# Who makes the low parts of the weight chunks: GpSimd, or VectorE from the first gated v chunk on

## The chip, the cores and the metric

One core of a Trainium2 chip runs the whole program in one launch. The metric is the device time of that launch in microseconds; the kernel before was timed three times.

## What is computed

`x` is 256 tokens by 1024 (fp32). Two layers of a first block run, then two layers of a second. Only the end of the second block's layer matters here, the feed-forward part with learned experts:

```python
def chunk(xc):                       # 128 tokens at a time
    q = (xc @ w_q).reshape(c, PEER_HEADS, 2, PEER_HALF)
    sc = jnp.einsum('chpd,hpnd->chpn', q, sub_keys)
    ...                              # top 16 of 128 keys per half, then top 16 of the 256 pairs
    gate = jax.nn.softmax(best_s, axis=-1)
    act = jax.nn.gelu(jnp.einsum('chkd,cd->chk', u_tab[idx], xc))
    return jnp.einsum('chk,chkd->cd', gate * act, v_tab[idx])
```

There are 128 x 128 experts, each with a row of `u_tab` and of `v_tab` (1024 numbers each), 8 heads and 16 experts a head and token.

## The kernel before, in words

**No gathering.** The kernel doesn't fetch the chosen experts. It computes all 16,384 hidden values of every token densely, in 128 blocks of 128 experts, multiplies them by a gate that is zero where an expert was not chosen, and multiplies the result with all of `v_tab`. Block n needs a *u chunk* (128 x 1024, way in) and a *v chunk* (128 x 1024, way out).

**Three products for one.** Each fp32 operand is kept as a high part (rounded to the type that TensorE reads) and a low part (the rest), and a product is three matmuls: high by high, high by low, low by high (`mm3`). So each of the 800 weight chunks of 512 KB goes through: SyncE loads it into one of `RAW2` = 4 slots of `raw` (L462, by `load_layer`), ScalarE copies it to `w_hi` (L1077, class `Split`), GpSimd subtracts to get `w_lo` (L572, `split_layer`), TensorE uses both. Counting semaphores order this: `w_ready` (loaded), `hi_ready`, `lo_ready`, `w_used` (TensorE is done with n chunks). A raw slot is loaded again once `lo_ready` says that its low part is made; a pair of slots (`PAIR2` = 4) is written again once `w_used` says so. In the trace `w_hi` and `w_lo` are both named `w_split`.

**The order of chunks** in a layer of the second block: the first `N2_PRE` chunks are for projections and queries; then 48 u chunks (`STASH`), whose hidden values go, through Gelu, to a stash (`stash_in`) while VectorE still works on the top 16; then, from chunk `N2_OUT` on, 48 v chunks for these blocks; then, for blocks 48 to 127, u and v chunks in turn, each u one block ahead of its v (`run_base`, `_stream2`).

**The stages of the way out** (`RUNS`, L1308, L1927 and TensorE's `hidden_blocks`, L716):
- blocks 0 to 47 use the stash: one v chunk a block, and beside it one group of one-hots;
- blocks 48 to 95: a u and a v chunk, and one group of one-hots;
- blocks 96 to 127: a u and a v chunk.

**One block, engine by engine.** VectorE first makes a group of one-hots for gates that are needed 32 blocks later (`onehots`, L1900: `one_j` 256 wide, `one_i` 1024 wide, three `gate_j` 256 wide, all bf16), then in `gated` (L1420) the product of hidden values and gate twice (L1428 in fp32, L1429 as `hidw_hi`) and their difference `hidw_lo` (L1431). `gated` waits for `hid_ready` (Gelu done) and for `w_used` (the block two before is through). TensorE, in each turn of `one_pass`, computes the way in of the next block (24 matmuls of 256 columns, L656), a gate group (24 small matmuls, L997, out of the one-hots) and the way out of this block (12 matmuls of 512 columns, L656), which waits for `hidw_ready`. ScalarE makes the high parts of the next u and this v chunk, the Gelu (L1121) and a copy of the gates (L1279). The order of each engine is written out by hand in loops of its own, four blocks to a turn. GpSimd does nothing else in them than to split.

**GpSimd's part** is one program of its own, `split_layer(n, raws, pairs, pause, between)`: it goes through all `n` = `N2` chunks of the layer, in order, and waits for the matching counts. The rest of a layer's small work for GpSimd is done at chunk `pause`.

The lines that say it:

```python
pool.wait_ge(hi_ready, c + 1)
if at >= pairs:
    pool.wait_ge(w_used, c - pairs + 1)
pool.tensor_tensor(w_lo[at % pairs], raw[:, at % raws, :], w_hi[at % pairs].bitcast(F32),
                   ALU.subtract).then_inc(lo_ready, 1)
```

Of the kernel before, what the change touches and what calls it, by code (L numbers as in the profile page):

```python
# [22 lines left out]
F32 = mybir.dt.float32  # L23
# [4 lines left out]
ALU = mybir.AluOpType  # L28
# [29 lines left out]
NK = 128  # L58
# [9 lines left out]
N2_MIX = 13 + 4 + 1  # L68
N2_PRE = N2_MIX + 8 + 16
STASH = 48  # L70
N2_OUT = N2_PRE + STASH

RUNS = ((0, JQ), (JQ, STASH - JQ), (STASH, 2 * JQ - STASH), (2 * JQ, JQ), (3 * JQ, JQ))
N2 = N2_PRE + 2 * NK
RAW1, PAIR1 = 3, 6
RAW2, PAIR2 = 4, 4
EARLY = 3
AHEAD = 2
# [9 lines left out]
def run_base(first):  # L88

    return N2_OUT + first if first < STASH else N2_PRE + 2 * first  # L90

# [59 lines left out]
def two_blocks_kernel(nc, x_in, pos_in, stream, col1, row1, col2, row2, small2, sub2, inv_in, out):  # L151
# [4 lines left out]
    with ExitStack() as ctx:  # L156
# [10 lines left out]
        raw = sb("raw", [P, max(RAW1, RAW2), CH])  # L167
        RING = max(PAIR1, PAIR2)
        w_split = sb("w_split", [P, 2 * RING, CH], F32R)
        w_hi = [w_split[:, k, :] for k in range(RING)]  # L170
# [359 lines left out]
        def _(pool):  # L530
# [35 lines left out]
            def split_layer(n, raws, pairs, pause, between):  # L566

                def one(c, at):
# [6 lines that stand above are left out]
                turn = max(raws, pairs)  # L575
                head = max(turn, pause)
                head += (n - head) % turn
                for c in range(head):
                    if between is not None and c == pause:
                        between()  # L580
                    one(c, c)
                if between is not None and pause == head:
                    between()
                with pool.Fori(0, (n - head) // turn) as i:
                    for k in range(turn):
                        one(i * turn + (head + k), head + k)
# [35 lines left out]
            second_constants()  # L622
            with pool.Fori(0, DEPTH) as l:
                enter_layer(pool, "pool", l + (1 + DEPTH))
                split_layer(N2, RAW2, PAIR2, N2_MIX + AHEAD, mix_norm)
                leave_layer(pool, "pool", lo_ready, N2)

        CONSTS = 4
# [722 lines left out]
        def _(dve):  # L1351
            V = nc.vector
# [67 lines left out]
            def gated(i, unroll, u, done, base, ups, value, gate, free):  # L1420

                s = u % 2
                dve.wait_ge(hid_ready, i * unroll + (done + u + 1))
                if free:

                    first = isinstance(i, int) and i == 0 and u < 2
                    dve.wait_ge(w_used, base + u - 1 if first else i * (unroll * (ups + 1)) + (base + (ups + 1) * (u - 1) + ups))
                V.tensor_tensor(gated_hid[:, s, :], value, gate, ALU.mult).then_inc(gate_step, 1)  # L1428
                V.tensor_tensor(hidw_hi[:, s, :], value, gate, ALU.mult).then_inc(gate_step, 1)  # L1429
                dve.wait_ge(gate_step, i * (2 * unroll) + 2 * (done + u + 1))  # L1430
                V.tensor_tensor(hidw_lo[:, s, :], gated_hid[:, s, :], hidw_hi[:, s, :].bitcast(F32),  # L1431
                                ALU.subtract).then_inc(hidw_ready, 1)
# [185 lines left out]
            def layer_norm(step, n, full, dst, g, b, stats, mean_var, std, rstd, signal):  # L1618

                half = lambda c: slice(c * 512, (c + 1) * 512)  # L1620
                for count, banks in full:
                    dve.wait_ge(out_full, count)
                    for t, c in banks:
                        step(V.scalar_tensor_tensor(out=dst[:, t, half(c)], in0=x_res[:, t, half(c)], scalar=ALPHA,
                                                    in1=acc[2 * t + c], op0=ALU.mult, op1=ALU.add))
                    step.settle()
                    for t, c in banks:
                        step(V.bn_stats(stats[:, t, c, :], dst[:, t, half(c)]))
                step.settle()
                for t in range(TT):  # L1630
                    step(V.bn_aggr(mean_var[:, t, :], stats[:, t].rearrange("p c s -> p (c s)")))
                root_of(step, n)
                step(V.reciprocal(rstd, std))
                step.settle()
                for t in range(TT):
                    step(V.scalar_tensor_tensor(out=dst[:, t, :], in0=dst[:, t, :], scalar=mean_var[:, t, 0:1], in1=g,
                                                op0=ALU.subtract, op1=ALU.mult))
                    step.settle()
                    ins = V.scalar_tensor_tensor(out=x_res[:, t, :], in0=dst[:, t, :], scalar=rstd[:, t:t + 1], in1=b,
                                                 op0=ALU.mult, op1=ALU.add)  # L1640
                    if signal is not None:
                        ins.then_inc(signal, 1)
                    else:
                        step(ins)

            def block2():
# [253 lines left out]
                def onehots(n, i, step, free):  # L1900

                    if free:
                        dve.wait_ge(onehot_used, i * step + (n - 1))
                    s, q = n % 2, n // JQ
                    at = i * (step * GROUP) + n % JQ * GROUP
                    tokens = slice(at, at + GROUP) if isinstance(i, int) else bass.ds(at, GROUP)
                    pairs = lambda x: x.rearrange("p (c k) -> p c k", k=2)
                    shape = lambda keys: [P, GROUP // 2, keys, 2]
                    keys = iota_b[:, q * JQ:(q + 1) * JQ, :]
                    V.tensor_tensor(one_j[:, s], keys.unsqueeze(1).broadcast_to(shape(JQ)),  # L1910
                                    pairs(i2T[:, tokens]).unsqueeze(2).broadcast_to(shape(JQ)),
                                    ALU.is_equal).then_inc(onehot_step, 1)
                    V.tensor_tensor(one_i[:, s], iota_b[:].unsqueeze(1).broadcast_to(shape(NK)),  # L1913
                                    pairs(i1T[:, tokens]).unsqueeze(2).broadcast_to(shape(NK)),
                                    ALU.is_equal).then_inc(onehot_step, 1)
                    dve.wait_ge(onehot_step, i * (2 * step) + 2 * (n + 1))
                    for m in range(PIECES):
                        ins = V.tensor_tensor(gate_j[:, s, :, m], one_j[:, s],  # L1918
                                              pairs(g_part[:, m, tokens]).unsqueeze(2).broadcast_to(shape(JQ)), ALU.mult)
                    ins.then_inc(onehot_ready, 1)  # L1920

                for u in range(8):
                    onehots(u, 0, 8, u >= 2)
                with dve.Fori(1, JQ // 8) as i:
                    for u in range(8):
                        onehots(u, i, 8, True)
                for first, n in RUNS:  # L1927
                    def one(i, u, free):
                        if first < NK - JQ:
                            onehots(JQ + first + u, i, 4, True)  # L1930
                        j = i * 4 + (first % JQ + u)
                        b = i * 4 + (first % JQ + u)
                        if first >= STASH:
                            value = hid[:, u % 2, :]
                        elif isinstance(b, int):
                            value = stash[first // JQ][:, b, :]
                        else:
                            value = stash[first // JQ][:, bass.ds(b, 1), :].rearrange("p b t -> p (b t)")
                        gated(i, 4, u, first, run_base(first), int(first >= STASH), value, gates[:, first // JQ % 2, :, j], free)

                    if first % JQ == 0:
                        dve.wait_ge(gates_out, first + JQ)
                    for u in range(4):
                        one(0, u, first > 0 or u >= 2)
                    with dve.Fori(1, n // 4) as i:
                        for u in range(4):
                            one(i, u, True)
                layer_norm(step, 6, [(LAST_SUMS - TT + t + 1, [(t, c) for c in range(2)]) for t in range(TT)], ypre,
                           par("ln2_g"), par("ln2_b"), bn3, mv3, std3, rstd3, None)
                return step.n  # L1950
# [122 lines left out]
```

## Time and profile before

| | |
|---|---|
| times of three runs | 3289.58, 3296.64, 3299.37 us |
| median | 3296.64 us |
| span of the profiled execution | 3291.1 us |
| TensorE matmuls busy | 2821.9 us (86%) |
| VectorE busy | 2427.6 us (74%), 3941 instructions |
| GpSimd busy | 2063.1 us (63%), of which 2028.4 us are the 800 splits |
| ScalarE busy | 1233.0 us (37%) |
| granted TensorE clock, mean over the span | 0.918 |
| read from HBM | 429 MB, 131 GB/s over the span |

The span runs from the first to the last instruction of one profiled execution; the three times are of runs of their own, their median 5.5 us above that span. Busy time counts an instruction from its start to its end, so one that stands still inside it counts as busy. The granted clock is a share of the full 2.4 GHz and is a mean of two levels, 1.2 and 2.4 GHz. A share over the whole span mixes stages with different limits, so the rows further down go stage by stage. "Idle before" in a row, in brackets, is the wait of the engine just before the instruction and who ended it.

### The profile page before, as it was taken

The numbers are of one execution on the slowest core, as the hardware profiler recorded it, in microseconds if no ns is written. First come the engines' busy times: TensorE is split into PE (matmuls) and PEld (weight loads), VectorE is DVE, ScalarE is ACT, GpSimd is POOL, SyncE is SP. The second block draws the span as 40 slices with busy tenths as digits, with TensorE's granted clock in tenths as the row PEclk, the third lists the DMA queues.
The fourth block names the chain that finished last, engine by engine and source line by source line (L and its number), as shares of the span: only waits on it lengthen the run. The fifth ranks groups of instructions, "written<-read, shape, count | busy, mean of one in ns | idle before, by whom it ended". The sixth has DMA issues, their size and how long they took to land.

```text
span 3291.1 us, 62310 instructions
## 1 busy us (share of the span) xinstructions
PE 2821.9 (86%) x21856; PEld 2498.9 (76%) x21856; DVE 2427.6 (74%) x3941; ACT 1233.0 (37%) x1814; POOL 2063.1 (63%) x849
## 2 busy tenths in 40 slices
PE   6899888999799777788888898789777788888897
PEld 6689877898589766568777787679765567777786
DVE  8521383313859999989999665849999989999766
ACT  4444343443435332223333343344432223333343
POOL 6378673887268544457667786357744447666786
PEclk9999997999699988789999999789998889999999
DMA  4145341555144322234434454224332224444453
GB/s 170 58 163 189 138 149 56 178 183 206 39 141 166 104 95 96 96 103 141 141 140 138 156 172 179 90 97 168 120 103 96 94 85 141 141 140 140 145 175 121
DMA packets 118027, 432.35 MB, mean 131 GB/s; under 512 B 13952, under 2 KB 13952, under 8 KB 117376
## 3 DMA queue, kind: packets, MB, share of 16 engines
q1 hardware_dynamic: 117888, 430.43, 37.8%
q8 instruction: 96, 1.57, 0.2%
q14 instruction: 43, 0.35, 0.0%
HBM read 429.33 MB, written 1.05 MB: 131 GB/s over the span
## 4 chain that ended last, share of the span: by engine, by line
PE 42%; DVE 37%; issue 16%; ACT 2%; DVEq 1%; POOL 1%; DMA 0%; SPq 0%; ACTq 0%; POOLq 0%
PE ps L656 40%; DVE hidw_hi L1429 7%; DVE hidw_lo L1431 5%; DVE gate_j L1918 4%; DVE one_i L1913 2%; DVE one_j L1910 2%; DVE arena L1428 2%; PE ps L997 2%; DVE arena L1852 1%; DVE arena L1874 1%; DVE arena L1877 1%; DVE arena L1844 1%; DVE arena L1837 1%; DVE arena L1838 1%; DVE arena L1495 1%
## 5 line engine op out<-in xcount | busy, mean ns | idle before, releaser
L572 POOL TENSOR_TENSOR w_split<-raw,w_split 128x1024 fp32r<-128x1024 f32 x800 | 2028.4, 2550 | 1008.5 <-ACT w_split L1077 1006.2
L656 PE MATMUL ps<-hT_hi,w_split 128*128 128x256 f32 x6688 | 1264.1, 286 | 22.9 <-POOL w_split L572 16.9
L1077 ACT ACTIVATE w_split<-raw 128x1024 fp32r<-128x1024 f32 x800 | 841.2, 1060 | 872.8 <-PE ps L656 698.6
L656 PEld LDWEIGHTS ps<-hT_hi,w_split 128*128 128x128 f32 x6688 | 1070.4, 193 | 39.3 <-POOL w_split L572 13.4
L656 PE MATMUL ps<-w_split,hidw_hi 128*128 128x512 f32 x2400 | 842.1, 434 | 186.8 <-DVE hidw_lo L1431 186.3
L656 PE MATMUL ps<-hT_lo,w_split 128*128 128x256 f32 x3344 | 952.0, 285 | 0.0
L656 PEld LDWEIGHTS ps<-w_split,hidw_hi 128*128 128x128 f32 x2400 | 470.9, 206 | 295.2 <-DVE hidw_lo L1431 129.4
L656 PEld LDWEIGHTS ps<-hT_lo,w_split 128*128 128x128 f32 x3344 | 646.2, 193 | 8.2
L1431 DVE TENSOR_TENSOR hidw_lo<-arena,hidw_hi 128x256 fp32r<-128x256 f32 x300 | 502.7, 1676 | 10.3
L656 PE MATMUL ps<-w_split,hidw_lo 128*128 128x512 f32 x1200 | 508.1, 423 | 0.0
L1918 DVE TENSOR_TENSOR gate_j<-one_j,arena 128x256 bf16<-128x256 bf16 x768 | 389.6, 561 | 31.4
L1428 DVE TENSOR_TENSOR arena<-arena 128x256 f32<-128x256 f32 (+1 forms) x224 | 179.0, 799 | 182.6 <-ACT arena L1121 167.5
L656 PEld LDWEIGHTS ps<-w_split,hidw_lo 128*128 128x128 f32 x1200 | 246.9, 206 | 62.0
L1429 DVE TENSOR_TENSOR hidw_hi<-arena 128x256 fp32r<-128x256 f32 (+1 forms) x224 | 283.0, 1263 | 0.0
L997 PEld LDWEIGHTS ps<-gate_j,one_i 128*128 128x128 bf16 x6144 | 172.8, 98 | 124.7 <-DVE gate_j L1918 73.9
L997 PE MATMUL ps<-gate_j,one_i 128*128 128x32 bf16 x6144 | 197.6, 178 | 76.5 <-DVE gate_j L1918 76.5
L656 PE MATMUL ps<-w_split,hT_hi 128*128 128x512 f32 (+1 forms) x704 | 223.2, 400 | 25.3 <-DVE arena L1505 14.7
L1428 DVE TENSOR_TENSOR arena<-arena,ps 128x256 f32<-128x256 f32 x44 | 18.5, 421 | 299.6 <-ACT arena L1121 299.6
L1121 ACT ACTIVATE arena<-ps 128x256 f32<-128x256 f32 x204 | 78.1, 383 | 418.3 <-PE ps L656 418.3
L656 PEld LDWEIGHTS ps<-w_split,hT_hi 128*128 128x128 f32 x704 | 137.8, 203 | 57.2 <-DVE arena L1505 15.5
L1913 DVE TENSOR_TENSOR one_i<-iota_b,i1T 128x1024 bf16<-128x1024 bf16 x256 | 174.3, 681 | 0.0
L1279 ACT COPY arena<-ps 128x256 f32 (+1 forms) x256 | 94.2, 368 | 195.1 <-PE ps L997 129.8
(210 smaller groups left out, 1898.2 us busy)
## 6 DMA issues: line engine op xcount, KB each, us to landing
raw<-in_stream SPq DMA_DIRECT2D x800, 512.0 KB, 3.2
row_sb<-in_row SPq DMA_DIRECT2D x2, 2306.0 KB, 11.5
arena<-in_sub SPq DMA_DIRECT2D x2, 1024.0 KB, 11.1
arena<-in_small SPq DMA_DIRECT2D x2, 640.0 KB, 8.9
x_res<-in_x SPq DMA_DIRECT2D x1, 1024.0 KB, 4.9
out_x<-x_res SPq DMA_DIRECT2D x1, 1024.0 KB, 4.0
row_sb<-in_row SPq DMA_DIRECT2D x2, 297.0 KB, 3.9
col_sb<-in_col SPq DMA_DIRECT2D x2, 40.5 KB, 3.1
```

The costliest lines, as they stand in the source:

```text
L572: pool.tensor_tensor(w_lo[at % pairs], raw[:, at % raws, :], w_hi[at % pairs].bitcast(F32), ALU.subtract).then_inc(lo_ready, 1)
L656: ins = nc.tensor.matmul(o, lhsT, rhs, start=start, stop=stop)
L997: ins = nc.tensor.matmul(b[:, k * JQ:(k + 1) * JQ], one_i[:, s, k // 2, :, k % 2], gate_j[:, s, k // 2, m, :, k % 2], start=m == 0, stop=m ...
L1077: A(w_hi[c % self.pairs], raw[:, slot, :], ACT.Copy).then_inc(hi_ready, 1)
L1121: A(hid[:, u % 2, :], ps[:, at_bank + u % 2, 0:SEQ], func).then_inc(hid_ready, 1)
L1279: nc.scalar.copy(gates[:, n // JQ % 2, tokens, :], ps[:, 6 + n % 2, 0:GROUP * JQ].rearrange("p (t j) -> p t j", t=GROUP)).then_inc(gates_o ...
L1428: V.tensor_tensor(gated_hid[:, s, :], value, gate, ALU.mult).then_inc(gate_step, 1)
L1429: V.tensor_tensor(hidw_hi[:, s, :], value, gate, ALU.mult).then_inc(gate_step, 1)
L1431: V.tensor_tensor(hidw_lo[:, s, :], gated_hid[:, s, :], hidw_hi[:, s, :].bitcast(F32), ALU.subtract).then_inc(hidw_ready, 1)
L1910: V.tensor_tensor(one_j[:, s], keys.unsqueeze(1).broadcast_to(shape(JQ)), pairs(i2T[:, tokens]).unsqueeze(2).broadcast_to(shape(JQ)), ALU. ...
L1913: V.tensor_tensor(one_i[:, s], iota_b[:].unsqueeze(1).broadcast_to(shape(NK)), pairs(i1T[:, tokens]).unsqueeze(2).broadcast_to(shape(NK)), ...
L1918: ins = V.tensor_tensor(gate_j[:, s, :, m], one_j[:, s], pairs(g_part[:, m, tokens]).unsqueeze(2).broadcast_to(shape(JQ)), ALU.mult)
```

## The change

From chunk `N2_SPLIT` = `N2_OUT` + 2 on, VectorE makes the low parts, with the same subtraction and the same two waits; GpSimd's `split_layer` stops before that chunk. In the blocks of the stash VectorE's `split` makes, behind block n's products, v chunk n + 2. In the later blocks it makes v chunk n and u chunk n + 2 behind block n's products. Ahead of the first block VectorE waits until GpSimd has made its last chunk. The last block has nothing left to split, so the last turn of the last loop is written out apart.

```diff
+N2_SPLIT = N2_OUT + 2
...
-                split_layer(N2, RAW2, PAIR2, N2_MIX + AHEAD, mix_norm)
+                split_layer(N2_SPLIT, RAW2, PAIR2, N2_MIX + AHEAD, mix_norm)
...
+                def split(c, i=0, step=0):
+
+                    dve.wait_ge(hi_ready, i * step + (c + 1))
+                    dve.wait_ge(w_used, i * step + (c - PAIR2 + 1))
+                    V.tensor_tensor(w_lo[c % PAIR2], raw[:, c % RAW2, :], w_hi[c % PAIR2].bitcast(F32),
+                                    ALU.subtract).then_inc(lo_ready, 1)
+
...
+                dve.wait_ge(lo_ready, N2_SPLIT)
                 for first, n in RUNS:
-                    def one(i, u, free):
+                    def one(i, u, free, final=False):
...
                         gated(i, 4, u, first, run_base(first), int(first >= STASH), value, gates[:, first // JQ % 2, :, j], free)
+                        if first < STASH:
+                            split(N2_SPLIT + first + u, i, 4)
+                        elif not final:
+                            split(run_base(first) + 2 * u + 2, i, 8)
+                            split(run_base(first) + 2 * u + 3, i, 8)
 
...
-                    with dve.Fori(1, n // 4) as i:
+                    last_pass = n // 4 - (first + n == NK)
+                    with dve.Fori(1, last_pass) as i:
                         for u in range(4):
                             one(i, u, True)
+                    if first + n == NK:
+                        for u in range(4):
+                            one(last_pass, u, True, u == 3)
```

## Rows read from the trace of the kernel before

**Rows 1.** Windows: length; busy PE, PEld, DVE, ACT, POOL; clock; DMA; GB/s

```profile
1194.00:1457.00 263.00, 208.86 (x1720) 159.37 (x1721) 242.16 (x384) 63.59 (x95) 114.73 (x46) 0.81 0.28 94
1457.00:1817.00 360.00, 317.63 (x2862) 283.66 (x2861) 342.84 (x379) 135.49 (x191) 252.59 (x96) 0.98 0.41 140
1817.00:2018.00 201.00, 185.15 (x1172) 165.69 (x1169) 122.93 (x98) 78.48 (x97) 159.31 (x63) 0.99 0.46 158
2713.00:3074.00 361.00, 320.64 (x2878) 285.97 (x2876) 343.61 (x381) 135.14 (x191) 250.54 (x96) 0.97 0.41 140
```

**Rows 2.** Timeline of VectorE: start us, us, then what ran

```profile
1193.75 0.60 DVE L1428 TENSOR_TENSOR arena<-arena 128x256 f32<-128x256 f32 x1
...
1817.09 0.43 DVE L1431 TENSOR_TENSOR hidw_lo<-arena,hidw_hi 128x256 fp32r<-128x256 f32 x1
...
2017.76 0.43 DVE L1431 TENSOR_TENSOR hidw_lo<-arena,hidw_hi 128x256 fp32r<-128x256 f32 x1
```

**Rows 3.** Waits of TensorE in stage A: us in total, times, longest

```profile
PE ps L656 <- DVE hidw_lo L1431: 43.3, 16, 3.5
```

**Rows 4.** Timeline in stage A: a split and a subtraction

```profile
1265.16 2.41 POOL L572 TENSOR_TENSOR w_split<-raw,w_split 128x1024 fp32r<-128x1024 f32 x1 [7.08 <-ACT w_split L1077]
...
1265.31 2.54 DVE L1431 TENSOR_TENSOR hidw_lo<-arena,hidw_hi 128x256 fp32r<-128x256 f32 x1
```

**Rows 5.** Durations, ns min/median/max, of two forms on VectorE

```profile
L1431 DVE TENSOR_TENSOR hidw_lo<-arena,hidw_hi x300: 424/2456/2655, 203.9 to 3272.7; 128x256 fp32r<-128x256 f32 x150
...
L1428 DVE TENSOR_TENSOR arena<-arena,ps x44: 420/422/423, 203.1 to 768.9; 128x256 f32<-128x256 f32 x44
```

**Rows 6.** Timeline of VectorE in stage A, no split beside it

```profile
1452.26 0.28 DVE L1910 TENSOR_TENSOR one_j<-iota_b,i2T 128x256 bf16<-128x256 bf16 x1
...
1453.98 0.64 DVE L1428 TENSOR_TENSOR arena<-w_split,arena 128x256 f32 x1
...
1455.20 0.43 DVE L1431 TENSOR_TENSOR hidw_lo<-arena,hidw_hi 128x256 fp32r<-128x256 f32 x1
1455.55 0.28 DVE L1910 TENSOR_TENSOR one_j<-iota_b,i2T 128x256 bf16<-128x256 bf16 x1
```

**Rows 7.** Timeline of TensorE: gate groups and first u matmuls

```profile
1451.71 0.77 PE L997 MATMUL ps<-gate_j,one_i 128*128 128x32 bf16 x24
...
1455.37 0.77 PE L997 MATMUL ps<-gate_j,one_i 128*128 128x32 bf16 x24
...
1605.41 0.77 PE L997 MATMUL ps<-gate_j,one_i 128*128 128x32 bf16 x24
...
1608.90 0.28 PE L656 MATMUL ps<-hT_hi,w_split 128*128 128x256 f32 x1
...
1611.78 0.77 PE L997 MATMUL ps<-gate_j,one_i 128*128 128x32 bf16 x24
...
1848.04 0.28 PE L656 MATMUL ps<-hT_hi,w_split 128*128 128x256 f32 x1
...
1853.70 0.28 PE L656 MATMUL ps<-hT_hi,w_split 128*128 128x256 f32 x1
```

**Rows 8.** VectorE's groups by form: busy us, mean ns

```profile
L1874 DVE TENSOR_TENSOR arena<-iota_k,arena 128x2048 f32<-128x2048 f32 x8 | 35.1, 4390 | 0.3
...
L1799 DVE TENSOR_TENSOR arena<-arena,row_sb 128x512 f32<-128x512 f32 x2 | 1.4, 692 | 0.1
```

**Rows 9.** ScalarE: the high parts, and a gate copy in stage B

```profile
L1077 ACT ACTIVATE w_split<-raw 128x1024 fp32r<-128x1024 f32 x800 | 841.2, 1060 | 872.8 <-PE ps L656 698.6
...
1612.71 0.37 ACT L1279 COPY arena<-ps 128x256 f32 x1 [0.28 <-PE ps L997]
```

**Rows 10.** Timeline of TensorE in stage A at the low clock

```profile
1258.42 1.22 PE L656 MATMUL ps<-w_split,hidw_hi 128*128 128x512 f32 x2 [2.78 <-DVE hidw_lo L1431]
...
1263.71 0.86 PE L997 MATMUL ps<-gate_j,one_i 128*128 128x32 bf16 x24
```

**Rows 11.** Busy time in the stretch ahead of stage A

```profile
1105.00:1190.00 85.00, 68.06 (x1131) 65.50 (x1129) 79.75 (x159) 32.72 (x64) 36.02 (x15) 0.98 0.28 96
```
## The prediction

> **What bounds the kernel now.** The profiled execution spans 3291.1 us; the three times have a median of 3296.6 us, 5.5 us more, so what the span loses the time loses. The last stretch of each second-block layer, the 128 weighted outputs (blocks from here on), is the only one that the diff touches, and it takes 824 of the 3291 us in each of two layers. I first cut it by what a block holds. Stage A: 48 blocks with one v chunk and one set of one-hots each. Stage B: 48 blocks with a u chunk, a v chunk and one-hots. Stage C: 32 blocks with u and v only. In [rows 1] see that VectorE is busy 92% of A and 95% of B while TensorE is at 79% and 88%; in C TensorE has 92% and VectorE 61%; and that layer two repeats layer one (only its stage B is shown). The stages' edges on VectorE: the first product starts at 1193.7, the last B block's hidw_lo at 1817.1 and the last C block's at 2017.8 [rows 2]; the last A block's ends at 1455.6 [rows 6]. That gives 261.9 / 48 = 5.46 us a block in A, 361.9 / 48 = 7.54 in B, 200.7 / 32 = 6.27 in C.
>
> Then who is waited for: TensorE waits longest for hidw_lo, VectorE's last instruction of a block, 43.3 us in A alone [rows 3]. Is VectorE really working when "busy"? [Rows 4] says no: a 128x256 subtraction that starts 0.15 us after GpSimd's split lasts 2.54 us and ends 0.3 us after it. [Rows 5] gives that line 424 ns at best and 2456 at the median, while the line that takes one operand from PSUM never exceeds 423 ns. So a VectorE instruction with both operands in SBUF stands still while GpSimd splits, and the 92 to 95% are largely such standing. Without it a block's whole VectorE work is the cycle in [rows 6]: one_j at 1452.26 to one_j at 1455.55, 3.29 us, with product, product and difference (1.5 us) in its second half.
>
> **What TensorE alone would need**, at the full clock: in A a block is 3.66 us, gate group to gate group; in B 6.37; in C 5.66, first u matmul to first u matmul [rows 7]. Against 5.46, 7.54 and 6.27 now, all three stages hold time that is VectorE's and GpSimd's doing.
>
> **The change part by part.**
> *Removed:* 206 splits a layer (256 - 48 - 2) from GpSimd, 412 of its 800. GpSimd then does nothing while VectorE works in these stages, so the standing still goes too.
> *Added:* the same 206 on VectorE: one per block in A, two in B and C. No row shows this instruction there. The nearest: a contiguous two-operand 128x512 fp32 takes 692 ns [rows 8] and the 128x256 one 424 [rows 5], so 268 ns more for 256 elements, and 1024 make 692 + 2 x 268 = 1228 ns, hence 1.23 us. The upper end is the slowest two-operand rate in the trace, 4390 ns for 2048 elements with broadcast operands [rows 8], 2.2 us for 1024; a lower end than 2 x 0.54 = 1.1 us (the streaming part alone) has no row. I take 1.23, since hidw_lo has the same types and layout as the split. VectorE's instructions overlap their neighbours by some 0.08 us, and two waits with register targets give that back: 1.23 each.
> *Sum, stage A:* 3.29 + 1.23 = 4.5 us on VectorE against 3.66 on TensorE. VectorE stays the bound, now with real work: 48 x 4.5 = 216 against 261.9, a gain of 46.
> *Stage B:* 3.29 + 2 x 1.23 = 5.75 against TensorE's 6.37: the bound passes to TensorE. 48 x 6.37 = 306, 3 for the first u chunk, for which nothing runs beside, and 0.3 for each of 12 turns of the loop: 313 against 361.9, a gain of 49.
> *Stage C:* 1.5 + 2.5 = 4.0 against 5.66: 32 x 5.66 = 181 plus 5 for the turns and the last block, 186 against 200.7, a gain of 15.
> Together 110 a layer, 220 in all: 3297 - 220 = **3077 us**.
>
> **Waits that the change adds, costed at nothing, and their cover.** A split waits on VectorE for ScalarE's high part and for a free low slot; behind it stand the next one-hots and products, for which TensorE waits. *A:* block n splits chunk n+2. Its slot is free, and ScalarE starts its part (1.06 us, [rows 9]), when block n-2's matmuls end; that is the wait that product n already made. Cover: more than a block. *B,* with S the start of block n's u matmuls: they end 2.88 us later [rows 7], ScalarE's Gelu and gate copy follow to S + 4.2 [rows 9], and the high part of the next u chunk is there at S + 5.3. VectorE's products and difference follow the Gelu, so they are over by S + 5.8, v chunk n is split by 7.0, and only then comes the u chunk, long ready, to 8.2. TensorE needs v chunk n at S + 6.37 + 2.88 + 0.6 = S + 9.9, so there are 2.9 us of cover; the u chunk it needs later still. If that cover went, each late microsecond would cost 48 a layer. *SyncE's queue:* a raw slot is refilled once its low part is made, in B and C now in pairs by S + 7.0 and 8.2. The load lands in 3.2 us and ScalarE asks for it at S + 12.7 (B) or 11.3 (C), so the loads stay hidden; the rate rises to 1.05 MB / 5.66 us = 185 GB/s, which the steady part of C has already. *The new wait for chunk N2_SPLIT - 1* before the first product: that chunk is two ahead of the first product's in every queue. At worst it is one split of GpSimd, 2.4 us a layer; I take nothing. *The last pass unrolled:* more code, no more work.
>
> **Where the clock stands.** In A the granted clock averages 0.81 [rows 1], that is 38% of the time at 1.2 GHz; there a block's matmuls and gate group take 1258.42 to 1264.4, 6.0 us [rows 10], more than 4.5. It falls around waits such as the 2.8 us for hidw_lo there. After the change the wait per block is below 1 us, and the stretch just before A, with TensorE 80% busy, was granted 0.98 [rows 11]; 3.66 / 4.5 is 81%. So I take the full clock.
> The Trainium skill (TensorE: Matmul & The Clock Gate, "A second HAM failure mode") reports a kernel whose clock kept swinging because TensorE idled briefly but often between groups of matmuls; by that rule the share at the low level could stay, and the sum would be the first rival's.
>
> **Rivals.**
> (1) *The clock in A stays as it is.* Then blocks run at 4.5 us for 62% of the time and 6.0 for 38%: 1 / (0.62/4.5 + 0.38/6.0) = 5.0 us, 24 a layer more: 3125. For it: the clock does swing there now. Against: rows 11, and a slow TensorE makes itself the bound, which leaves it no idle time. 0.12.
> (2) *The splits come late,* VectorE standing in order for ScalarE behind TensorE, and B and C give nothing: only A's 2 x 46 is left, 3205. Against: the cover above. 0.10.
> (3) *Slower: VectorE becomes the bound everywhere,* because the 128x1024 split runs at the slow rate of rows 8, 2.2 us. A: 3.29 + 2.2 = 5.5; B: 3.29 + 4.4 = 7.7, C under its 6.27. 48 x 0.04 + 48 x 0.16 = 10 a layer, 3315. It decides from about 2.1 us a split. Against: contiguous rows of both nearer sizes. 0.04.
> (4) *The change doesn't relieve VectorE,* the long durations being a trait of these operands and not GpSimd's doing. Then 1.23 or 2.46 us is added to a full engine: far slower, 3450. Rows 5 and 6 have the same line at 424 ns. 0.01.
>
> **How the numbers follow.** Forecast 0.73. Its own bounds: the wait at the start 0 to 2.4 a layer, a split of 1.1 to 1.4 us moves A by 6 to 8 a layer; B and C could have 0.2 us more a block of loop turns and issue gaps (16 a layer): 3050 to 3120. The lower end goes to 3040 in case VectorE overlaps more; the upper to 3140 takes in rival 1. That leaves out rivals 2 to 4 and the forecast's tails, some 0.2. About 0.3% is what a measurement of this kernel can tell from no change. Faster: all but rivals 3 and 4 and a remainder of 0.01: 0.94; same 0.02; slower 0.04.
>
> **What would show it.** Right: the new line on VectorE at 1.2 us x412; GpSimd with 388 splits; hidw_lo at 424 ns throughout blocks 0 to 127; the stages at 216, 313 and 186 us; TensorE over 95% busy in B and C and waiting for VectorE only in A; the clock above 0.95 in A. Wrong: a split above 1.5 us (B turns VectorE-bound), TensorE's waits in B naming the new line (rival 2), or 0.8 as the clock in A (rival 1).

## The result, and the profile after

The changed kernel takes 3019.6 us in the median of four runs (3012.7 to 3027.2), the kernel before 3293.1 (3287.7 to 3299.4): ratio 0.9175, 95% interval 0.9143 to 0.9207, 8% less. Timed once more, four times beside two other versions, it came at 0.9218 (0.9187 to 0.9249). The forecast was 3077 us with a range of 3040 to 3140: right in sign and in mechanism, 57 us too high, and the measured time lies below the range.

The profiled run spans 3025.1 us, 266 less than before. Its groups by cost, from the page of the changed kernel; columns are busy us, mean ns, then idle time before and who ended it:

```profile
PE 2713.4 (90%) x21856; PEld 2426.4 (80%) x21856; DVE 2165.6 (72%) x4353; ACT 1232.1 (41%) x1814; POOL 1006.0 (33%) x437
...
L574 POOL TENSOR_TENSOR w_split<-raw,w_split 128x1024 fp32r<-128x1024 f32 x388 | 971.2, 2523 | 1106.6 <-ACT w_split L1079 1105.6
...
L1928 DVE TENSOR_TENSOR w_split<-raw,w_split 128x1024 fp32r<-128x1024 f32 x412 | 489.1, 1218 | 10.3 <-ACT w_split L1079 10.3
```

VectorE has 412 instructions more and is busy 262 us less. An engine that gets 489 us of new work and ends up less busy had been counting something else as work before. What, the durations of `hidw_lo` say (instructions that write or read this tile, changed kernel; ns min/median/max):

```profile
L1433 DVE TENSOR_TENSOR hidw_lo<-arena,hidw_hi x300: 424/425/2316, 203.9 to 3006.5; 128x256 fp32r<-128x256 f32 x150
```

The median of [rows 5], 2456 ns, is 425 now. Busy time by stretch for A, B and C, columns as in [rows 1], the edges moved to where the stages now lie:

```profile
1192.00:1396.00 204.00, 173.52 (x1692) 134.57 (x1692) 195.98 (x423) 64.25 (x93) 0.00 (x0) 0.99 0.36 121
1397.00:1700.00 303.00, 303.00 (x2849) 275.17 (x2849) 256.62 (x478) 133.48 (x191) 0.00 (x0) 1.00 0.50 165
1701.00:1884.00 183.00, 182.48 (x1180) 164.53 (x1179) 124.29 (x160) 77.68 (x97) 0.00 (x0) 1.00 0.54 176
```

TensorE is busy in all of B and in 99.7% of C, at the full clock; in A it is at 85% and VectorE at 96%, now with work. TensorE still waits for VectorE in A, in short pieces (waits of TensorE in stage A, changed kernel: us in total, times, longest; against [rows 3], 43.3 us in 16 waits of up to 3.5):

```profile
PE ps L658 <- DVE hidw_lo L1433: 30.7, 45, 1.0
```

In B and C the profile has no wait of TensorE for VectorE, but for one of 0.7 us at the edge, for the difference of A's last block. Measured from the first `hidw_lo` start of a layer to the 48th, the 96th and the 128th, both layers alike within 2 us:

| us per layer | A | B | C | sum |
|---|---|---|---|---|
| before | 260.3 | 361.9 | 200.7 | 822.9 |
| after | 204.2 | 304.0 | 183.2 | 691.5 |
| less | 56.1 | 57.9 | 17.5 | 131.4 |

Twice 131 is 262 of the 266 us. The rest is the start of the first product, 2.9 us sooner in the first layer. Of these, 0.8 are there already before the one-hots begin, in a part that the change doesn't touch. The other 2.1, and 1.8 in the second layer, come from the last group of one-hots ahead of the product: before, its three `gate_j` took 2.84 us beside a split, and now they take 0.69. Timeline of VectorE in stage A of the changed kernel, one block and the start of the next:

```profile
1387.78 1.22 DVE L1928 TENSOR_TENSOR w_split<-raw,w_split 128x1024 fp32r<-128x1024 f32 x1
1388.91 0.28 DVE L1912 TENSOR_TENSOR one_j<-iota_b,i2T 128x256 bf16<-128x256 bf16 x1
1389.11 0.68 DVE L1915 TENSOR_TENSOR one_i<-iota_b,i1T 128x1024 bf16<-128x1024 bf16 x1
1389.94 0.69 DVE L1920 TENSOR_TENSOR gate_j<-one_j,arena 128x256 bf16<-128x256 bf16 x3
1390.63 0.63 DVE L1430 TENSOR_TENSOR arena<-w_split,arena 128x256 f32 x1
1391.18 0.61 DVE L1431 TENSOR_TENSOR hidw_hi<-w_split,arena 128x256 fp32r x1
1391.82 0.42 DVE L1433 TENSOR_TENSOR hidw_lo<-arena,hidw_hi 128x256 fp32r<-128x256 f32 x1
1392.16 1.22 DVE L1928 TENSOR_TENSOR w_split<-raw,w_split 128x1024 fp32r<-128x1024 f32 x1
```

The split lasts 1.22 us, but the next instruction starts 1.13 after it: what a split costs VectorE is the second number.

### The profile page after: what moved, and what is told of

Its sections match the earlier page's. It is cut to its first block and busy times, and to the rows that moved or that the text cites. A ratio compares the mean times of both kernels' runs of the same rounds, so it can differ in the third digit from the quotient of the medians.

```text
span 3025.1 us, 62006 instructions
## 1 busy us (share of the span) xinstructions
PE 2713.4 (90%) x21856; PEld 2426.4 (80%) x21856; DVE 2165.6 (72%) x4353; ACT 1232.1 (41%) x1814; POOL 1006.0 (33%) x437
## 5 line engine op out<-in xcount | busy, mean ns | idle before, releaser
L574 POOL TENSOR_TENSOR w_split<-raw,w_split 128x1024 fp32r<-128x1024 f32 x388 | 971.2, 2523 | 1106.6 <-ACT w_split L1079 1105.6
L658 PE MATMUL ps<-w_split,hidw_hi 128*128 128x512 f32 x2400 | 774.6, 404 | 63.9 <-DVE hidw_lo L1433 62.9
L658 PEld LDWEIGHTS ps<-w_split,hidw_hi 128*128 128x128 f32 x2400 | 429.8, 189 | 155.4 <-DVE hidw_lo L1433 50.3
L1928 DVE TENSOR_TENSOR w_split<-raw,w_split 128x1024 fp32r<-128x1024 f32 x412 | 489.1, 1218 | 10.3 <-ACT w_split L1079 10.3
L658 PE MATMUL ps<-w_split,hidw_lo 128*128 128x512 f32 x1200 | 473.2, 394 | 0.0
L1430 DVE TENSOR_TENSOR arena<-arena 128x256 f32<-128x256 f32 (+1 forms) x224 | 142.9, 638 | 183.9 <-ACT arena L1123 183.1
L658 PEld LDWEIGHTS ps<-w_split,hidw_lo 128*128 128x128 f32 x1200 | 225.8, 188 | 55.4
L1920 DVE TENSOR_TENSOR gate_j<-one_j,arena 128x256 bf16<-128x256 bf16 x768 | 241.8, 369 | 31.4 <-DVE one_i L1915 0.2
L1433 DVE TENSOR_TENSOR hidw_lo<-arena,hidw_hi 128x256 fp32r<-128x256 f32 x300 | 141.5, 472 | 10.3
```

The source lines that it names most:

```text
L658: ins = nc.tensor.matmul(o, lhsT, rhs, start=start, stop=stop)
L1920: ins = V.tensor_tensor(gate_j[:, s, :, m], one_j[:, s], pairs(g_part[:, m, tokens]).unsqueeze(2).broadcast_to(shape(JQ)), ALU.mult)
L1928: V.tensor_tensor(w_lo[c % PAIR2], raw[:, c % RAW2, :], w_hi[c % PAIR2].bitcast(F32), ALU.subtract).then_inc(lo_ready, 1)
```

## The experiments

All start from the changed kernel. `early` and `both` ran four times, the others once. The stage times are again between `hidw_lo` starts of the profiled run, first layer; the second was within 1.2 us everywhere. A second profiled run of the changed kernel gave 204.3, 304.1 and 183.2, so a difference of 1 us in a stage can be told; the spans scatter by more, as the last section shows.

| run | A | B | C | span |
|---|---|---|---|---|
| changed kernel | 204.2 | 304.0 | 183.2 | 3025.1 |
| a_only | 204.1 | 363.1 | 201.0 | 3175.9 |
| bc_only | 260.6 | 304.3 | 183.2 | 3142.0 |
| pool_sub | 306.3 | 485.8 | 252.3 | 3762.0 |
| pool_set | 204.3 | 304.1 | 183.2 | 3015.7 |
| dbl_a | 261.9 | 305.6 | 183.2 | 3137.6 |
| dbl_b | 204.1 | 325.4 | 181.6 | 3061.2 |
| dbl_c | 204.2 | 304.0 | 186.0 | 3034.3 |
| scal | 177.4 | 306.7 | 183.2 | 2973.2 |
| early | 204.2 | 304.0 | 183.2 | 2979.3 |
| both | 176.1 | 305.6 | 183.2 | 2932.9 |

**Half of the change at a time.** `a_only`: VectorE splits in A, then GpSimd goes on, with the same subtraction for the chunks from `back` to N2 - 1.

```diff
                 split_layer(N2_SPLIT, RAW2, PAIR2, N2_MIX + AHEAD, mix_norm)
+                back = N2_OUT + STASH + 2
+                pool.wait_ge(lo_ready, back)
...
-                        elif not final:
-                            split(run_base(first) + 2 * u + 2, i, 8)
-                            split(run_base(first) + 2 * u + 3, i, 8)
```

> VectorE makes the low parts of stage A's chunks alone; from stage B's first split on GpSimd makes them again. If each stage's gain is its own (theory), A stays at 204 us as after the change and B and C go back to 362 and 200: 3025 + 2 x (58 + 17) = 3175 us of span. If what was gained in B and C came from the state in which A hands over (TensorE's clock, chunks ahead of their use), B and C stay below 330 and 190 and the span is under 3120.

`bc_only`: GpSimd splits through A, VectorE from B on.

```diff
-N2_SPLIT = N2_OUT + 2
+N2_SPLIT = N2_OUT + STASH + 2
...
-                        if first < STASH:
-                            split(N2_SPLIT + first + u, i, 4)
-                        elif not final:
+                        if first >= STASH and not final:
+                            if first == STASH and isinstance(i, int) and i == 0 and u == 0:
+                                dve.wait_ge(lo_ready, N2_SPLIT)
```

> GpSimd makes the low parts through stage A, VectorE from stage B on. Theory: A 260 us and clock 0.81 as before, B 304, C 183: 3025 + 2 x 56 = 3137 us of span. Rival (A's slow clock and late low parts are handed on): B above 310.

Both came as the theory has it, each stage to about 1 us: a stage has the time that goes with whoever splits in it and takes nothing from its neighbour. The span of bc_only, 3142.0, is 5 us above the 3137 of the theory, which had left out the start of the first product: that comes 2.3 us later again than in the changed kernel. The clock goes with the stage too (busy time by stretch of bc_only, A then B; columns as in [rows 1]):

```profile
1194.00:1454.00 260.00, 204.56 (x1670) 156.06 (x1667) 238.71 (x376) 62.87 (x93) 114.95 (x46) 0.81 0.28 95
1455.00:1759.00 304.00, 304.00 (x2874) 276.17 (x2874) 255.75 (x478) 134.35 (x192) 2.40 (x1) 1.00 0.49 164
```

**Is it GpSimd's being busy, or the split itself?** `pool_sub` leaves all splits on VectorE and gives GpSimd useless work of the same kind:

```diff
+                def spend(c, k, i=0):
+                    pool.wait_ge(hi_ready, i * 4 + (c + 1))
+                    for j in range(3):
+                        pool.wait_ge(idle_step, i * 12 + (3 * k + j))
+                        pool.tensor_tensor(absd[:], after[:], before[:], ALU.subtract).then_inc(idle_step, 1)
```

> The kernel after the change, and beside it GpSimd does, for each chunk that it no longer splits, three 128x384 subtractions of two SBUF tiles that nobody uses (about 1 us each). Theory (a VectorE instruction with two SBUF operands and a GpSimd one exclude each other): VectorE's instructions stand still again, hidw_lo's median is above 800 ns, A goes above 250 us, B above 340, and the span above 3250 us, though every split is still VectorE's. Rival (the gain is that the low part takes 1.2 us and not 2.5, or comes in VectorE's own order): nothing changes, 3020 to 3030 us.

It was the largest effect of the study, 737 us more, and far beyond the 3250 that I had named: three subtractions a chunk can hit VectorE three times, and VectorE now has its own splits besides. The median of `hidw_lo` is 1108 ns. Timeline of pool_sub in stage A, rows of the two engines:

```profile
1232.88 2.38 POOL L634 TENSOR_TENSOR absd<-after,before 128x384 f32<-128x384 f32 x2
1233.28 1.11 DVE L1447 TENSOR_TENSOR hidw_lo<-arena,hidw_hi 128x256 fp32r<-128x256 f32 x1
1234.31 2.03 DVE L1942 TENSOR_TENSOR w_split<-raw,w_split 128x1024 fp32r<-128x1024 f32 x1
```

The 424 ns subtraction takes 1.11 us and the 1.22 us split 2.03: each stands until a subtraction of GpSimd ends. The rival (only the shorter split counts) said 3020 to 3030 and is out. The trace of the kernel before speaks against it too: at every wait for `hidw_lo` in the three stages GpSimd's latest split had ended 0.3 us or more before TensorE went on, and VectorE's difference 0.05 to 0.15 us before, so the low part was never what came last.

`pool_set` lets GpSimd write only, but for one 128x1 subtraction a chunk that carries the waits:

```diff
+                    pool.wait_ge(idle_step, i * 20 + 5 * k)
+                    pool.tensor_tensor(absd[:, 0:1], absd[:, 0:1], absd[:, 0:1], ALU.subtract).then_inc(idle_step, 1)
+                    for dead in (absd[:, 1:], after[:], before[:], rel[:]):
+                        pool.memset(dead, 0.0).then_inc(idle_step, 1)
```

> The same with GpSimd writing only: for each chunk four fills of 128x384 (0.42 us each) behind a 128x1 subtraction. If only reads exclude each other, as the Trainium skill says (SBUF - State Buffer, Who interferes with whom), the stages stay at 204, 304 and 183 us and hidw_lo at 424 ns. If any GpSimd instruction on SBUF does it, VectorE stands still some 1.7 us a chunk: A above 240 and the span above 3150 us.

The stages didn't move. Timeline of pool_set in stage A:

```profile
1230.87 1.22 DVE L1943 TENSOR_TENSOR w_split<-raw,w_split 128x1024 fp32r<-128x1024 f32 x1
1230.90 1.23 POOL L633 TENSOR_TENSOR absd<-absd 128x1 f32<-128x1 f32 x1 [1.76 <-ACT w_split L1094]
...
1232.42 0.42 POOL L635 MEMSET after<- 128x384 f32 x1
1232.78 0.42 POOL L635 MEMSET before<- 128x384 f32 x1
1233.03 0.70 DVE L1935 TENSOR_TENSOR gate_j<-one_j,arena 128x256 bf16<-128x256 bf16 x3
1233.15 0.42 POOL L635 MEMSET rel<- 128x384 f32 x1
1233.64 0.62 DVE L1445 TENSOR_TENSOR arena<-arena 128x256 f32 x1
```

Fills of 0.42 us run beside gate_j and a product, and neither side is longer than alone. This version gives GpSimd more instructions a chunk than pool_sub, each with its semaphore step (five against three), so these are not what cost the time there. And the one-element-wide subtraction of GpSimd, 0.19 us at its shortest, takes 1.23 here: it came 30 ns after VectorE's split and stood until that was over. So the exclusion works in both directions. It holds for bf16 as well as fp32, as the durations of `one_j` say (two bf16 operands in SBUF; ns min/median/max, pool_sub and then pool_set):

```profile
L1926 DVE TENSOR_TENSOR one_j<-iota_b,i2T x256: 275/283/1127, 1089.4 to 3467.7; 128x256 bf16<-128x256 bf16 x128
...
L1927 DVE TENSOR_TENSOR one_j<-iota_b,i2T x256: 275/284/294, 1094.6 to 2810.2; 128x256 bf16<-128x256 bf16 x128
```

The Trainium skill says this of the pair of ports that the two engines share (SBUF — State Buffer, "Who interferes with whom"): a VectorE instruction with two SBUF inputs contends with a GpSimd instruction that reads SBUF, not with one that only writes it, and whichever is first holds for its whole length. Both runs agree: 1108 against 425 ns for the median of `hidw_lo`, and 1.23 against 0.19 us for the small subtraction.

**Which engine bounds each stage now.** Three kernels make one split twice in one stage: `more` has the two waits and the subtraction of `split`, and counts up `twice`:

```diff
+                def more(c, i, step, k):
...
+                    dve.wait_ge(twice, i * 4 + (k + 1))
...
+                            more(N2_SPLIT + first + u, i, 4, first + u)
                             split(N2_SPLIT + first + u, i, 4)
```

> In stage A each split is made twice on VectorE, the second behind the first. Theory (VectorE's own work bounds A at 4.3 us a block): 1.28 us more a block, A 204 -> 266 us, B and C unchanged. Rival (A is held by TensorE or by the order of waits, with slack on VectorE): A below 230. With 2 us of wait a block TensorE's clock should show whether it falls with such waits: below 0.9 if so.

> In stage B the v chunk's split is made twice. Theory (TensorE bounds B at 6.34 us a block, VectorE has 5.4 us of work there): 5.4 + 1.28 = 6.7 us, so VectorE just becomes the bound and B goes from 304 to 318 us, not by 61. Rival (VectorE is the bound of B as well): 365.

> In stage C the v chunk's split is made twice. Theory: 4.0 + 1.28 = 5.3 us of VectorE under TensorE's 5.66, so C stays at 183 us. Rival: C above 200.

In A the second split costs in full, 57.7 / 47 = 1.23 us a block (1.28 expected): VectorE is the bound. In C the same addition costs 2 to 3 us in all where a VectorE-bound stage would lose 40. In B it costs 21.4 us, between the 14 of the theory and the 61 of the rival: a block is 6.78 us instead of the 6.68 that the theory adds up to. There the cover of the raw loads ends too, which I had not expected (waits of ScalarE in stage B of dbl_b):

```profile
ACT w_split L1080 <- DMA raw<-in_stream: 79.2, 44, 3.8
```

A split that comes later frees its raw slot later. Whether these waits make the 0.1 us was not settled.

TensorE's clock in dbl_a's A was 0.89: it went back and forth between the two levels all through the stage. There its waits were short and of two kinds (waits of TensorE in stage A of dbl_a):

```profile
PE ps L1000 <- DVE gate_j L1921: 29.2, 30, 1.2
PE ps L659 <- DVE hidw_lo L1434: 29.0, 46, 0.8
```

**Taking work off VectorE in A.** `scal` lets ScalarE make the high part from the first product and puts the split between product and difference, where it covers ScalarE:

```diff
-                V.tensor_tensor(hidw_hi[:, s, :], value, gate, ALU.mult).then_inc(gate_step, 1)
-                dve.wait_ge(gate_step, i * (2 * unroll) + 2 * (done + u + 1))
...
+                    V.tensor_tensor(gated_hid[:, s, :], value, gate, ALU.mult).then_inc(gate_step, 2)
+                    between()
+                    dve.wait_ge(high_ready, i * unroll + (done + u + 1))
...
+                                act.wait_ge(gate_step, i * 8 + 2 * (first + u + 1))
+                                A(hidw_hi[:, u % 2, :], gated_hid[:, u % 2, :], ACT.Copy).then_inc(high_ready, 1)
```

> In stage A the second product (hidw_hi, 0.53 us of VectorE a block) is replaced by a copy of the first on ScalarE (0.38 us), and VectorE splits between the product and the difference. If VectorE's 4.29 us bound A, a block falls to 3.76 and A from 204 to 181 us; TensorE's 3.66 is just below. If the order of waits (PE for hidw_lo, VectorE for ScalarE) bounds it, A stays above 200.

A fell to 177.4 us, 3.77 a block. TensorE is now at its own limit there as well (busy time by stretch, A of scal):

```profile
1189.00:1365.00 176.00, 172.48 (x1692) 134.41 (x1692) 165.51 (x374) 82.38 (x143) 0.00 (x0) 0.98 0.43 141
```

**Starting sooner, and both together.** `early` moves the handover 16 chunks up, beside the first 32 groups of one-hots:

```diff
-N2_SPLIT = N2_OUT + 2
+N2_SPLIT = N2_PRE + JQ + 2
...
+                def split_beside(u, i=0):
+                    if u % 2:
+                        split(N2_SPLIT + u // 2, i, 4)
```

> The changed kernel again, for the ratio in the same job as the two below: 0.9175 of before within 0.004, and a span of either about 3011 or about 3025 us, since the runs so far came at these two.

> VectorE also makes the low parts of the 16 u chunks that lie beside the first 32 groups of one-hots (GpSimd stops 16 chunks sooner). There a u chunk and two groups took 5.4 us, with VectorE standing still behind GpSimd; its own work is 2 x 1.55 + 1.13 = 4.3 us and TensorE's 2.9 + 1.3 = 4.2. Theory: 16 x 1.1 = 17 us a layer, 34 us less than the changed kernel. Rival (the stretch is bound by the order of waits between TensorE, ScalarE and VectorE): less than 10 us in all.

> The two versions together: the earlier start and, in stage A, hidw_hi by ScalarE. If the gains are each stage's own they add: 34 + 48 = 82 us less than the changed kernel, 2930 to 2945 us, ratio to before 0.89 to 0.895.

Medians of four runs each: changed kernel 3031.4 us, early 2984.7 (ratio to before 0.9086, 0.9051 to 0.912), both **2938.7** (0.8944, 0.8918 to 0.8971). Between the end of stage C of the first layer and the first `hidw_lo` of the second, early takes 414.2 us and the changed kernel 431.3: 17.1 less, as expected. Twice that is 34 of early's 47 us; the rest lies ahead of the second block and belongs to the scatter shown at the end. The gains add stage by stage (A 28 us less a layer, B 1.6 more, the start 17 less), and `both` beats the kernel before by 10.6%. That it fell inside the 2930 to 2945 us expected is in part luck: the changed kernel's median was 3031 this time and not 3025, its ratio just outside the 0.9175 within 0.004 that I had named, and `both` lies 93 us below it where 82 were expected.

## Why the prediction was right, and where it was wrong

**Right:** that VectorE's long durations were standing and not work, and GpSimd's splits the cause (pool_sub); the split at 1.23 us (1218 ns); which engine bounds which stage (dbl_a, dbl_c); that the splits would not come late (v and u chunk, in B and C: no wait of TensorE for them), that the loads stay hidden in the changed kernel, and that the order of the gains would be B, A, C. Rivals 2, 3 and 4 are out with these.

**The first rival, the clock:** 0.99 in A. 45 waits of up to 1.0 us in 204 us did not bring it down, so in the changed kernel nothing is seen of the rule that I quoted (short but frequent idling may keep the clock swinging). In dbl_a it is seen: no wait of TensorE was longer than 1.2 us, but there were 76 of them, 58 us of 259 in all, and the clock swung and averaged 0.89. With the waits of up to 3.5 us of the kernel before it averaged 0.81 [rows 1]. So short waits went either way in this kernel, and the rival was a real one. What decides between the two cases was not tried.

**Wrong:** the size, 220 us where the spans show 266. With the stage edges of the prediction the terms stand like this:

| term, us per layer | forecast | measured | too high by |
|---|---|---|---|
| A | 216 | 205.8 | 10 |
| B | 313 | 303.6 | 9 |
| C | 186 | 183.2 | 3 |
| start of the first product | no gain | 2.1 sooner (1.8 in the second layer) | 2 |

- *A: "3.29 + 1.23 = 4.5 us", times 48.* The cycle is 204.2 / 47 = 4.34 us. A split costs 1.13 where it stands in a row of instructions; I had taken that overlap back for "two waits with register targets", which cost nothing that shows. The cycle without it is then 3.21: I had read one of the longest cycles as the typical one. And between those edges lie 47 whole cycles and a piece, not 48.
- *B and C: "0.3 for each of 12 turns of the loop", "3 for the first u chunk" and "5 for the turns and the last block".* These allowances have nothing behind them. TensorE's own 48 x 6.37 + 32 x 5.66 = 487 us is what B and C together take, 486.8. In the changed kernel the first u matmuls of successive blocks start 6.37 us apart in B and 5.66 in C, over the turns of the loop too, so the turns cost nothing. The first u chunk is one of the 80 that this sum counts already, and the last block's way out lies behind the edge.
- *The start:* I had looked only for a loss there (0 to 2.4 us) and not for the same relief as elsewhere.

Together with the start that is the 46 us of span by which the forecast fell short (266 against 220), all with one sign: each doubtful term was rounded towards a smaller gain, and the range (3040) was then laid around the rounded sum, with 3050 as the best that the terms allowed. Stage A at 4.3 and the bare sum of TensorE for B and C would have given 3034. The remaining 11 us of the 57 are scatter: the median of before was 3.5 us lower in this comparison, and the medians differ by 7.5 us more than the two profiled spans do.

## What to carry to other kernels

Before an elementwise operation is given to GpSimd because VectorE is "busy", look at min and median of VectorE's instructions with two SBUF operands: a median that comes near the length of GpSimd's instruction is standing, and taking the work over can be cheaper than sharing it. Then make the sum for each stage from the shortest cycle that repeats, and leave out allowances for which no row shows a cost in a stage where nothing waits; put them in the range instead. The next step is to look which stage is still VectorE's and to move from there what has one operand, as the high parts here, to ScalarE.

## What the runs showed of the hardware that I had not expected

*A fork ahead of everything.* The profiled run of the changed kernel spans 3025.1 us and pool_set's 3015.7, and a stretch that neither version touches, in the second layer of the first block, explains it. Busy time there in the changed kernel's profiled run:

```profile
500.00:577.00 77.00, 64.96 (x277) 53.48 (x276) 27.04 (x95) 29.06 (x74) 25.53 (x14) 0.74 0.15 48
```

and in pool_set's:

```profile
500.00:577.00 77.00, 59.63 (x311) 50.24 (x311) 34.30 (x109) 34.59 (x86) 26.89 (x15) 0.88 0.16 55
```

The same instructions run at a granted clock of 0.74 or 0.88 and end 12 us apart, of which 10 are left at the start of the second block's work. What decides it was not tried. The changed kernel's four runs beside the kernel before spanned 3010.5, 3011.5, 3023.3 and 3025.1, which looks like the same two cases; but its next four, for which I had expected about 3011 or about 3025, spanned 3021.1, 3025.8, 3032.8 and 3033.7, so two cases are not all of the scatter. A difference of 12 us between two spans of this kernel is no evidence; the stage times, which repeated to 0.1 us in the changed kernel's two profiled runs, are.

*Two operands, two rates.* The comparison of 2048 elements in [rows 8] takes 2.1 ns an element (4390 ns for 2048) and the contiguous split 1.2 (1218 ns for 1024), both fp32 with two SBUF operands. The broadcast operand in rows of 16 is the visible difference; which part of it costs was not tried.
